# Six attention heads' softmax weights turned by VectorE and DRAM, with the last pair's products half a chunk later

## The reference

```
q, k: 6 heads x 2 maps of width 64;  v: 6 heads of width 128
logits = q k^T + bias[bucket(k_pos - q_pos)]          # two maps per head
probs  = softmax(logits)
w      = probs[:, 0] - lam * probs[:, 1]               # 256 x 256 per head
o      = rms_norm(w @ v, subln) * (1 - lam_init)
y      = concat(o, memory attention) @ w_o             # then layer norm of ALPHA*x + y
```

## Time and profile before

| | |
|---|---|
| median of three runs | 1242.42 us |
| the profiled execution | 1243.12 us |
| its span, first to last instruction | 1241.0 us |
| mean granted TensorE clock | 0.998 |
| TensorE busy | 1228.3 us (99%) |
| VectorE busy | 1037.2 us (84%) |
| ScalarE busy | 720.6 us (58%) |
| GpSimd busy | 26.8 us (2%) |
| the 16 DMA engines, share | 58.2% |

### The profile page before, as it was taken

The page is one execution under the profiler, slowest core; times in us unless marked ns, Lnnn a source line. Parts: engine busy times, 40 slices in busy tenths (PEclk is TensorE's granted clock), DMA queues, the critical chain, the costliest instruction groups (busy, mean ns, idle before and its releaser), DMA issues.

```text
span 1241.0 us, 19585 instructions
## 1 busy us (share of the span) xinstructions
PE 1228.3 (99%) x7290; PEld 1076.8 (87%) x7290; DVE 1037.2 (84%) x1613; ACT 720.6 (58%) x1170; POOL 26.8 (2%) x37
## 2 busy tenths in 40 slices
PE   9999999999999999999999999999999999999997
PEld 8988888888999998888889888888888988888886
DVE  6896888889779888988888978988888786988887
ACT  6674765555776546655554546655554674755552
POOL 0011000000000100000000000000000011000000
PEclk9999999999999999999999999999999999999999
DMA  9874575555553344656654774666555673666651
GB/s 339 278 235 160 189 249 190 187 187 169 170 184 123 119 148 166 227 191 201 189 187 170 246 255 167 223 200 194 192 187 174 210 238 113 225 205 199 198 190 53
DMA packets 79993, 239.75 MB, mean 193 GB/s; under 512 B 8694, under 2 KB 24694, under 8 KB 78876
## 3 DMA queue, kind: packets, MB, share of 16 engines
q1 hardware_dynamic: 79900, 238.51, 58.2%
HBM read 232.18 MB, written 6.30 MB: 192 GB/s over the span
## 4 chain that ended last, share of the span: by engine, by line
PE 92%; DVE 3%; ACT 2%; DMA 1%; issue 1%; SPq 1%; DVEq 0%; ACTq 0%
PE pair L844 29%; PE acc L938 21%; PE pair L847 14%; PE pair L876 4%; PE pair L877 3%; PE pair L878 3%; PE acc L844 2%; PE pair L1109 2%; PE acc L919 2%; PE acc L918 2%; PE acc L917 2%; DMA raw<-in_stream 1%; PE acc L847 1%; ACT ex L1304 1%; PE pair L1063 1%
## 5 line engine op out<-in xcount | busy, mean ns | idle before, releaser
L1365 DVE TENSOR_TENSOR w_lo<-raw,w_hi 128x1024 fp32r<-128x1024 f32 x400 | 482.5, 1221 | 89.7 <-ACT w_hi L1127 88.3
L1127 ACT ACTIVATE w_hi<-raw 128x1024 fp32r<-128x1024 f32 x400 | 419.9, 1057 | 220.1 <-PE pair L847 71.2
L844 PE MATMUL pair<-xT,w_hi 128*128 128x512 f32 x1520 | 478.0, 396 | 0.2 <-DVE w_lo L1365 0.2
L847 PEld LDWEIGHTS pair<-xT,w_lo 128*128 128x128 f32 x1520 | 285.6, 188 | 67.2
L847 PE MATMUL pair<-xT,w_lo 128*128 128x256 f32 x1520 | 298.9, 278 | 0.0
L844 PEld LDWEIGHTS pair<-xT,w_hi 128*128 128x128 f32 x1520 | 233.7, 189 | 3.5 <-DVE w_lo L1365 0.4
L1174 ACT ACTIVATE hid<-pair 128x512 f32<-128x512 f32 x88 | 52.6, 598 | 125.6 <-PE pair L847 125.6
L1406 DVE TENSOR_TENSOR hid<-pair,hid 128x512 f32<-128x512 f32 x88 | 60.6, 689 | 48.1 <-ACT hid L1174 47.7
L876 PE MATMUL pair<-xT,w_hi 128*128 128x256 f32 x336 | 97.4, 290 | 0.0
L877 PE MATMUL pair<-xT,w_hi 128*128 128x256 f32 x336 | 95.0, 283 | 0.0
L878 PE MATMUL pair<-xT,w_lo 128*128 128x256 f32 x336 | 95.0, 283 | 0.0
(11 more groups left out here) (229 smaller groups left out, 1654.3 us busy)
## 6 DMA issues: line engine op xcount, KB each, us to landing
raw<-in_stream SPq DMA_DIRECT2D x400, 512.0 KB, 4.7
gains<-in_ln SPq DMA_DIRECT2D x8, 1024.0 KB, 8.8
swap_scratch<-ex SPq DMA_DIRECT2D x24, 128.0 KB, 2.6
bias<-bias_scratch SPq DMA_DIRECT2D x2, 1152.0 KB, 8.3
raw<-in_stream SPq DMA_DIRECT2D x8, 256.0 KB, 6.0
swap_scratch<-prob SPq DMA_DIRECT2D x32, 64.0 KB, 4.3
a_sq<-swap_scratch SPq DMA_DIRECT2D x8, 256.0 KB, 2.9
xprobT<-swap_scratch SPq DMA_DIRECT2D x3, 512.0 KB, 3.9
```

Source lines behind the costliest of these rows:

```text
L844: pe.matmul(bank, w_hi[:, slot, kk * P:(kk + 1) * P], xT[:, kk].rearrange("p a s -> p (a s)"), start=(kk == 0), stop=(kk == KT - 1), skip_ ...
L847: last = pe.matmul(bank[:, 0:SEQ], w_lo[:, slot, kk * P:(kk + 1) * P], xT[:, kk, 0, :], start=False, stop=(kk == KT - 1), skip_group_check ...
L1127: nc.scalar.activation(w_hi[:, u % SPLIT, :], raw[:, u % RAW, :], ACT.Copy).then_inc(hi_ready, 1)
L1365: v.tensor_tensor(w_lo[:, u % SPLIT, :], raw[:, u % RAW, :], w_hi[:, u % SPLIT, :].bitcast(F32), ALU.subtract).then_inc(lo_ready, 1)
```

## The change

All six heads take the `swap`, `fetch`, `spread` way. `turnw` is gone from all engines. Heads 4 and 5 have their `exp`, `prob` and `swap` together between the halves of V1, ahead of the first `seed`; V2's second split stands after the chunk (`late_unit`) and after `scale` 0 and the fetch of head 4; `pv` of heads 4 and 5 stands between the halves of WO1 instead of after WO0, and `ms`, `tok` and `scale` of pair 2 come later too. `scale` 2 stands between the halves of WO2 instead of ahead of them. The squares of all pairs are written to one buffer, since the others are landing places of fetches.

```diff
-    def chunk(form, role, layer, index, between=(), after=(), held=False):
+    def chunk(form, role, layer, index, between=(), after=(), held=False, late_unit=False):
...
-        if not held and c > 1:
+        if not held and not late_unit and c > 1:
             split_units(2 * c + 1 + AHEAD)
...
         items.extend(after)
+        if late_unit:
+            split_units(2 * c + 1 + AHEAD)
...
-                  14: [it("pv", 0), it("pv", 1), it("ms", 0), it("exp", 4)],
-                  15: [it("tok", 0), ("seed", 2 * layer, 1), it("exp", 5), it("prob", 4)],
-                  16: [it("spread", 2)],
-                  17: [it("scale", 0), it("prob", 5), it("spread", 3)],
-                  18: [it("turnw", 4), it("pv", 2), it("pv", 3), it("turnw", 5)],
-                  19: [it("pv", 4), it("pv", 5), it("ms", 1), it("tok", 1), it("ms", 2)], 20: [it("scale", 1), it("tok", 2)],
-                  21: [it("scale", 2)]}
+                  14: [it("pv", 0), it("pv", 1), it("ms", 0), it("exp", 4), it("prob", 4), it("swap", 4), it("tok", 0),
+                       it("exp", 5), it("prob", 5), it("swap", 5)],
+                  15: [("seed", 2 * layer, 1)], 16: [it("spread", 2)], 17: [it("scale", 0), it("spread", 3), it("fetch", 4)],
+                  18: [it("pv", 2), it("pv", 3), it("fetch", 5), it("spread", 4)], 19: [it("ms", 1), it("tok", 1), it("spread", 5)],
+                  20: [it("pv", 4), it("pv", 5), it("scale", 1)], 21: [it("ms", 2), it("tok", 2)], 22: [it("scale", 2)]}
             at[14].append(("seed", 2 * layer, 0))
...
-                  held=role == "WO" and index[0] == 2)
+                  held=role == "WO" and index[0] == 2, late_unit=(role, index) == ("V", 2))
...
-            return ... if layer == 1 else a_sq[:, p, :]
+            return ... if layer == 1 else a_sq[:, 0, :]
...
-                        sp.wait_ge(head_landed, 4 * (item[1] // 3) + item[2] - 1)
+                        sp.wait_ge(head_landed, HEADS * (item[1] // 3) + item[2] - 1)
...
-                    if n in turned_ord:
-                        pe.wait_ge(probT_ready, turned_ord[n])
-                    else:
-                        pe.wait_ge(head_landed, 4 * (layer // 3) + h + 1)
+                    pe.wait_ge(head_landed, HEADS * (layer // 3) + h + 1)
...
                 elif name == "spread":
                     pool.wait_ge(swap_landed[n % 2], 16 * swap_count[n])
+                    if item[2] >= 4:
+                        pool.wait_ge(xpv_done, 2 * item[1] + 1)
```

More of the change, by code:

```diff
@@ L277, in trunk_kernel @@
     prob_ord = {(items[pos][0][:-4],) + items[pos][1:]: n for n, pos in enumerate(prob_pos)}
-    swap_count, swap_ord, turned_ord, seen = {}, {}, {}, {}
+    swap_count, swap_ord, seen = {}, {}, {}
     for item in items:
@@ L284, in trunk_kernel @@
             swap_ord[n] = len(swap_ord) + 1
-        elif item[0] == "turnw":
-            n = prob_ord["", item[1], item[2]]
-            turned_ord[n] = len(turned_ord) + 1
     def weights_of(item):
@@ L315, in trunk_kernel @@
             banks = (proj_ord[item[1]] % 2,)
-        elif name in ("turnw", "bias_rows"):
+        elif name == "bias_rows":
             banks = (0,)
@@ L482, in head_sq @@
         def head_sq(layer, p):
-            return QD[1][:, 2 * p:2 * p + 2, :].rearrange("p h s -> p (h s)") if layer == 1 else a_sq[:, p, :]
+            return QD[1][:, 2 * p:2 * p + 2, :].rearrange("p h s -> p (h s)") if layer == 1 else a_sq[:, 0, :]
         raw_landed = [sem(f"raw_landed{i}") for i in range(RAW)]
@@ L504, in trunk_kernel @@
         xprob_ready, xprob_turned, xprobT_ready, swapped = sem("xprob_ready"), sem("xprob_turned"), sem("xprobT_ready"), sem("swapped")
-        prob_ready, prob_turned, probT_ready = sem("prob_ready"), sem("prob_turned"), sem("probT_ready")
         head_landed = sem("head_landed")
@@ L592, in side_read @@
                 return sq_ready, pair_ord[item[1], item[2] if name == "hpv" else item[2] // 2] + 1
-            if name == "turnw":
-                return probT_ready, turned_ord[prob_ord["", item[1], item[2]]]
             return {"bias_rows": rows_ready, "xpv": xmix_ready}[name], u + 1
@@ L1020, in _ @@
                         last.then_inc(xprob_turned, 1)
[L1021 to L1032, removed]
                 elif name == "xpv":
@@ L1052, in _ @@
                     layer, h = item[1:]
-                    n = weights_of(item)
-                    if n in turned_ord:
-                        pe.wait_ge(probT_ready, turned_ord[n])
-                    else:
-                        pe.wait_ge(head_landed, 4 * (layer // 3) + h + 1)
+                    pe.wait_ge(head_landed, HEADS * (layer // 3) + h + 1)
                     pe.wait_ge(v_ready, values_of(layer, h // 2))
@@ L1313, in _ @@
                         nc.scalar.activation(xprobT[:, i * 512:(i + 1) * 512], side_bank(pos, i)[:], ACT.Copy).then_inc(xprobT_ready, 1)
[L1314 to L1317, removed]
                 elif (name == "pv" and item[2] % 2) or name == "hpv":
@@ L1618, in _ @@
                         before, layer, h = items[prob_pos[n - 2]]
-                        if before == "prob" and n - 2 in swap_count:
+                        if before == "prob":
                             dve.wait_ge(swap_stored[s], 64 * swap_count[n - 2])
-                        elif before == "prob":
-                            dve.wait_ge(prob_turned, turned_ord[n - 2])
                         elif n - 2 not in swap_count:
@@ L1646, in _ @@
                                                           prob[:, s, 1, t, :], ALU.mult, ALU.add)
[L1647 to L1650, removed]
+                        link(last)
                 elif name in ("xswap", "swap"):
```

## The result

| | before | after |
|---|---|---|
| median of all its runs | 1242.9 us (4 runs) | 1251.52 us (4 runs, 1249.94 to 1254.64) |
| the profiled execution | 1243.12 us, span 1241.0 | 1250.59 us, span 1248.8 |
| mean granted TensorE clock | 0.998 | 0.995 |

The ratio is 1.0074, interval 1.0062 to 1.0086: slower, outside the range given. A second set of runs of the same kernel had 1250.83 us, ratio 1.0063 [1.0050, 1.0077].

The account below looks back on a forecast made before the run. TensorE's own work, 92% of the span, was taken to bound the kernel. 7.47 us goes; 0.9, 1.2 and 5.3 come back, 7.4 together: -0.1, so 1243.0 us profiled, 1242.3 median, range 1239.0 to 1246.0.

Parts of the forecast that it names:

- step 3: Heads 4 and 5 by DRAM: fetch usable after 2.90 us; TensorE waits 0.8 us in layer 0, 0.4 in layer 3.
- What is removed: Around WO0: two turnings per layer, the stall and layer 0's low clock go, 4.73 and 2.74 us, 7.47 together.
- Step 1: Seeds: ScalarE does `exp` 5 ahead of both, so WO0 starts 0.6 us later in layer 0, 0.3 in layer 3.
- Step 2: VectorE's queue: split for WO0's second half done at 92.5, needed at 94.2; hidden, with 1.7 us of cover.
- head 5 comes late: Rival: SP's in-order queue puts head 5's fetch behind a load waiting for VectorE; TensorE loses 4.8 us more, 1247.1; 10%.
- Step 4: End of the projection, `pv` 4 to WO3: waits of 0.29, 1.8 and 0.55, 2.64 us per layer, 5.3 in both.
- The clock rival: Rival: TensorE's clock falls in the new waits, notably at `scale` 2; 1.58 us per layer, 1243.9 or 1245.5; 15%.
- three signs of being wrong: Wait at `scale` 2 under 1 us; VectorE's split for WO0 late; head 5's copy over 1.6 us after TensorE asks.

Follow-up runs that it names:

- experiment 1: Changed kernel without the stores and fetches of heads 4 and 5, GpSimd copying block-turned weights straight from VectorE's buffer (result not the reference's): 1241.77 us, ratio 0.9993.
- Experiments 3 and 4: Changed kernel with fetches of heads 4 and 5 ahead of three loads, or all loads: 1243.67, 1244.19 us; and with head 5's fetch behind one more load: 1254.49 us.
- experiment 3: Changed kernel, fetches of heads 4 and 5 moved earlier in SP's order: one load still ahead, 1243.67 us; no load ahead, 1244.19 us.

## Why the prediction was wrong

The step that failed is step 3, its fetch term: it took 2.90 us from issue to landing from a quiet stretch, with at most 0.8 more if a load slowed it, and where the new fetches run they took 4.2 to 6.6. What each step said and what the traces of the changed kernel show:

- *What is removed, 7.47.* Right: no stall and no `turnw` is left, and experiment 1, which removes the same, has 1241.8 us where the forecast without step 3 is 1242.3 - 1.2 = 1241.1.
- *Step 1, 0.9.* WO0 starts at 90.18 in layer 0, 0.5 later than said; in layer 3, counted with the 3.97 brought along, 0.25 earlier than before, where 0.3 later was said. Together 0.8: the sum is right because the misses cancel, which is luck.
- *Step 2, hidden.* Right: TensorE never waits for the split of WO0's second half, which is done at 92.9 (said: 92.5).
- *Step 3, 1.2, at most 1.6 per layer.* Measured 4.2 + 3.45 = 7.65, and the half clock behind it another 1.7 (11.71 and 11.46 against 10.72). The stores were out at 93.62 (said: 93.2); the fetch of head 5 went out at 98.22 (said: 97.1), as both fetches stand between loads; it landed after 6.3 (said: 2.90); the copies took 0.61 (said: the long time, up to 1.44, as they would fall among splits; VectorE was waiting just then). Of the 3.4 us by which head 5's wait is over the forecast's 0.8 in layer 0, nearly all is the landing: 6.3 - 2.90 = 3.4; the later issue (+1.1), the shorter copy (up to -0.8) and TensorE's own later arrival (-0.3) cancel. The rival *head 5 comes late* named the right place and the right neighbour, at 10%. Its price, 1.2 us more for the stores and 1.2 for the fetch in each layer, missed too: head 5's stores were out at 93.62 and its fetch did not have to wait for them, while the fetch alone took 3.4 us more in layer 0 and 3.7 in layer 3. All of it started from a fetch behind a queue that SP's own wait had emptied.
- *Step 4, 10.72 from `pv` 4 to WO3.* Experiment 1 has 10.73 in both layers. Single waits differ (1.53 at `scale` 2, 1.8 said; 0.33 at WO3, 0.55 said). The total is sound, the single waits partly a matter of counting: the rows count idle time from the modelled end of a matmul, some 0.2 us behind the next start that the sum counts from. In the changed kernel half clock makes the halves longer and takes up part of them (0.16 and 0.90 at `scale` 2).
- *The clock rival* came true as a follower: the fall came with the 2.28 and 2.45 us waits for head 5, not with the one at `scale` 2. In experiment 1 waits of 1.53 leave the clock at 1.00. The price of 1.58 per layer was too high for this place: it is 0.9, as longer halves first use up the wait at `scale` 2, 1.53 without half clock, that the chain by ScalarE and VectorE sets.

Two of the three signs of being wrong came: the wait at `scale` 2 was under 1 us in both layers, and the copy of head 5 ended over 1.6 us after TensorE asked for it. By its own terms the forecast is -0.7 in layer 0 and +0.6 in layer 3, not -0.8 and +0.7; measured are +3.97 and +3.69.

Together: 7.65 + 1.73 in place of 1.2 is 8.2 more; less about 0.2 for halves that run 0.1 us shorter than their units and 0.1 in step 1, that is 7.9, and the profiled execution came out 1250.59 - 1243.0 = 7.6 above its forecast. Experiments 3 and 4 show the cause from both sides.

## What to carry to other kernels

The latency of a transfer belongs to the traffic in front of it: read the DMA share and the queue's neighbours in the stretch where the new transfer will run, and where the only row of such a transfer comes from a quiet stretch, let the range reach to what the bulk loads themselves take in a full one (4.7 us in the median here, 4.9 to 7.0 in the stretches that counted). When latency-bound fetches and bulk loads share an in-order queue, put the fetch ahead of the loads, as far as the loads can bear it. A step that looks dear in the profile may be cheap work behind a dear wait: here ready work moved in front of it gave 3.9 us, and taking the work away, with the late order that came with it (experiment 1), nothing that can be measured.

## What the runs showed of the hardware

- The same 256 KB fetch by SP landed after 2.6 to 3.7 us where no load was issued between the stores and it (two fetches of the kernel before, engines at 0.60 and 0.63; four of experiment 3, at 0.50 to 0.81 from issue to landing), after 4.6 to 5.4 behind one load (four, at 0.89 to 0.96), after 4.2 to 7.3 behind two to four (eight in the changed kernel, twice profiled, at 0.97 to 1.03), and after 6.9 to 10.5 when ScalarE issued it in its own queue (four). By the Trainium skill, DMA: Bandwidth & Descriptors, Latency and other measured facts, access to HBM takes 0.2 us on average and up to 2 at high load; the rows here differ by more than these 2.
- TensorE's clock stayed at 2.4 GHz after idle stretches of 1.53, 1.65 and 1.72 us (the last in experiment 3), and was at 1.2 GHz after those of 2.02 (the second set of the changed kernel), 2.06, 2.28 and 2.45.
- GpSimd's 128x4 power step took 1.01 us while VectorE waited and 2.06 beside a two-input subtraction of VectorE.
